# Two tensors that TensorE reads, begun 64 bytes further on in a float32 kernel of eight layers

## The reference, cut to what matters

```python
y = x32 * lax.rsqrt(jnp.mean(x32 * x32, axis=-1, keepdims=True) + EPS)
...
return (jax.nn.silu(h @ wg) * (h @ wu)) @ wd          # feed-forward, 1024 -> 2816 -> 1024
...
proj = jnp.einsum("bsd,de->bse", h, w_in)             # hybrid layer, 1024 -> 3584
...
return x + jnp.einsum("bse,ed->bsd", y, w_out)
```

## Time and profile before

| | |
|---|---|
| median of 3 runs | 1328.5 us (1327.9 to 1328.56) |
| the profiled execution's own time | 1327.45 us |
| its span, first to last instruction | 1325.7 us |
| granted TensorE clock, mean | 0.994 of full speed (2.4 GHz) |
| TensorE matmul busy | 98% of the span |
| DVE, ACT, POOL busy | 68%, 53%, 12% |

### The profile page before, as it was taken

The page is one execution under the profiler, slowest core; times in us unless marked ns, Lnnn a source line. Parts: engine busy times, 40 slices in busy tenths (PEclk is TensorE's granted clock), DMA queues, the critical chain, the costliest instruction groups (busy, mean ns, idle before and its releaser), DMA issues.

```text
span 1325.7 us, 23603 instructions
## 1 busy us (share of the span) xinstructions
PE 1297.9 (98%) x9662; PEld 1219.8 (92%) x9662; DVE 901.2 (68%) x1588; ACT 709.0 (53%) x1149; POOL 153.5 (12%) x207
## 2 busy tenths in 40 slices
PE   9999899999999999999999999999999999999997
PEld 7788678999999988899999999999998889999997
DVE  6986698777665567867666566666547776766652
ACT  7663656564445476466444444454458545554441
POOL 3106510250000210003000011000110001200000
PEclk9999899999999999999999999999999999999999
DMA  8535443555555543245555655555655234555560
GB/s 320 192 106 170 158 168 114 186 175 180 189 190 177 191 146 125 90 132 194 182 179 180 203 180 191 186 179 177 203 164 175 65 128 128 193 177 188 182 198 35
DMA packets 61499, 221.77 MB, mean 167 GB/s; under 512 B 7120, under 2 KB 7376, under 8 KB 61136
## 3 DMA queue, kind: packets, MB, share of 16 engines
q1 hardware_dynamic: 60768, 219.00, 49.8%
q0 software_dynamic: 336, 1.11, 0.3%
q10 hardware_dynamic: 288, 0.16, 0.1%
HBM read 219.20 MB, written 1.05 MB: 166 GB/s over the span
## 4 chain that ended last, share of the span: by engine, by line
PE 80%; DVE 10%; POOL 4%; issue 3%; ACT 1%; DMA 1%; SPq 0%; DVEq 0%; ACTq 0%; POOLq 0%
PE pb L473 13%; PE pb L474 12%; PE pb L475 12%; PE pb L488 7%; PE pb L489 7%; PE pb L490 7%; PE pb L457 5%; PE pb L458 5%; PE pb L459 5%; DVE s_wl L1263 3%; DVE s_acc L1396 2%; PE pb L581 2%; PE pb L531 2%; PE pb L704 1%; PE pb L560 1%
## 5 line engine op out<-in xcount | busy, mean ns | idle before, releaser
L1263 DVE TENSOR_TENSOR s_wl<-s_wraw,s_wh 128x1024 fp32r<-128x1024 f32 (+1 forms) x411 | 505.6, 1251 | 114.4 <-ACT s_wh L882 114.3
L882 ACT ACTIVATE s_wh<-s_wraw 128x1024 fp32r<-128x1024 f32 (+1 forms) x411 | 420.5, 1047 | 199.3 <-PE pb L475 112.6
L473 PE MATMUL pb<-s_xh,s_wh 128*128 128x256 f32 x1408 | 399.5, 284 | 0.0
L475 PE MATMUL pb<-s_xh,s_wl 128*128 128x256 f32 x1408 | 398.8, 283 | 0.0
L474 PE MATMUL pb<-s_xl,s_wh 128*128 128x256 f32 x1408 | 398.8, 283 | 0.0
L474 PEld LDWEIGHTS pb<-s_xl,s_wh 128*128 128x128 f32 x1408 | 270.6, 192 | 0.0
L473 PEld LDWEIGHTS pb<-s_xh,s_wh 128*128 128x128 f32 x1408 | 270.5, 192 | 0.0
L475 PEld LDWEIGHTS pb<-s_xh,s_wl 128*128 128x128 f32 x1408 | 270.5, 192 | 0.0
L488 PE MATMUL pb<-s_hh,s_wh 128*128 128x256 f32 x704 | 194.8, 277 | 0.0
L490 PE MATMUL pb<-s_hh,s_wl 128*128 128x256 f32 x704 | 194.7, 277 | 0.0
L489 PE MATMUL pb<-s_hl,s_wh 128*128 128x256 f32 x704 | 194.7, 277 | 0.0
(11 more groups left out here) (302 smaller groups left out, 1516.2 us busy)
## 6 DMA issues: line engine op xcount, KB each, us to landing
s_wraw<-in_w SPq DMA_DIRECT2D x407, 512.0 KB, 4.1
s_nab<-in_rpb SPq DMA_DIRECT2D x2, 1024.0 KB, 9.4
s_x<-in_x SPq DMA_DIRECT2D x4, 256.0 KB, 5.9
out_dram<-s_at_s SPq DMA_DIRECT2D x4, 256.0 KB, 2.3
s_cst<-in_cst SPq DMA_DIRECT2D x1, 684.0 KB, 9.7
s_mlev<-in_lev POOLq DMA_DIRECT2D x1, 576.0 KB, 5.5
s_wraw<-in_w SPq DMA_DIRECT2D x2, 256.0 KB, 4.4
s_ln<-in_lng POOLq DMA_DIRECT2D x2, 128.0 KB, 7.0
```

The lines of the kernel that those rows point to most:

```text
L473: pe.matmul(o, wh[:, s, w], xh[:, k, :], start=k == v == 0, stop=False, skip_group_check=True)
L475: r = pe.matmul(o, wl[:, s, w], xh[:, k, :], start=False, stop=k == 7, skip_group_check=True)
L882: return act.activation(o, src, ACT.Copy, scale=scale)
L1263: dve.tensor_tensor(wl[:, s, part], wraw[:, r, part], wh[:, s, part].bitcast(F32), ALU.subtract).then_inc(low_done, 1)
```

## The change

Two unused tensors of 16 float32 are taken in the same memory, one ahead of `xh` and one behind `xl`:

```diff
     x = sb("x", [P, 8, TOKENS])
+    sb("gap0", [P, 16])
     xh = sb("xh", [P, 8, TOKENS], F32R)
     xl = sb("xl", [P, 8, TOKENS], F32R)
+    sb("gap1", [P, 16])
     cst = sb("cst", [P, NCST])
```

## The result

| | before | changed |
|---|---|---|
| median us | 1328.2 (4 runs, 1327.69 to 1328.56) | 1319.2 (4 runs, 1317.65 to 1320.94) |
| ratio | 1 | 0.9933, 95% interval 0.9916 to 0.995 |
| profiled execution: span | 1325.7 | 1319.1 |

What follows compares the result with a forecast made beforehand. TensorE's matmul-to-matmul distance was taken to bound the kernel. From 1327.45 us, 26.7 off for project_features after give-backs and 2.7 off for project_tokens gave 1298.0 us, 1299 at the median; range 1292 to 1321.

Steps and rivals of the forecast that it cites:

- The reading of the address: TensorE matmuls: held and moved operand reads collide when both start in the same half of 128 bytes, costing 6.7 ns each.
- The period of 128 bytes: Operand start addresses: only the remainder by 128 bytes counts, so shifting a tensor by 128 bytes costs nothing.
- Step 1: project_features: 4,224 matmuls go from 120.0 to 113.3 ns apart, saving 28.3 us.
- The second state: project_out sometimes ran near 118 ns instead of 113 after an interruption; 113 was expected behind spread's transposes in project_features.
- step 3: Between norm_sums and spread in the feed-forward layers: 120 matmuls run at 118 ns, 0.5 us less gain.
- The 118 state: Rival, chance 0.12: after norm_sums all of project_features runs at 118 ns, saving 8.3 us, giving 1320 us.
- Step 2: Start of feed-forward layers: norm_sums waits for POOL's sum, which gets no faster; together 1.1 us of gain given back.
- Step 4: project_tokens in b1 and mix: 6.7 ns less per matmul, mostly covered by other waits, 2.7 us gained.
- the other bound: project_tokens: 6.7 ns more for each of 1,344 matmuls, 9.0 us worse.
- Step 5: Everything from cst on moves by 128 bytes, and ACT's and DVE's writes of xh and xl change: no cost.
- The slower rival: Chance 0.08: pattern repeats after 256 bytes, project_out falls to 120 ns, 19.3 us lost, project_features gains nothing; 1348 us.
- Step 6: Weight supply and DVE in project_features keep up at the new pace, 2.72 us per weight unit; no new wait.

Runs made afterwards that it cites:

- x at 192: Against the kernel before, xh and xl start 192 bytes further on and everything behind xl 256 bytes further on; 1315.91 us, ratio 0.9908.
- its split: Against the kernel before, parts of xh and xl moved 192 bytes in the feed-forward layers alone, everything behind by 512; 1308.83 us, ratio 0.9864.
- wiping: Parts of xh and xl moved 192 bytes in feed-forward layers alone, but block 7 of 8 kept at distance 0 from wh and wl; 1306.96 us, ratio 0.9837.
- 32 bytes: Against the kernel before, xh and xl start 32 bytes further on and everything behind xl 256 bytes further on; 1322.4 us, ratio 0.9957.
- wiping with distance 64: As wiping, but blocks 0 to 6 of xh and xl at distance 64 from wh and wl in place of 192; 1320.29 us, ratio 0.9944.
- the kernel without the stop: As wiping, with norm_sums after 9 tiles in place of 7 and the spreads after 14 in place of 11, first feed-forward layer; 1301.93 us, ratio 0.9799.
- the first split: Parts of xh and xl at remainder 64 in feed-forward layers alone, 0 in b1 and mix; xl landed 128 bytes off xh by 256; 1322.11 us, ratio 0.9959.
- both wiping kernels: The two kernels wiping and the kernel without the stop, both with block 7 at distance 0; 1306.96 us and 1301.93 us.

## Why the prediction was right or wrong

In the profiled execution the forecast, 1298.0 us, was missed by 22.9 us. By the tables, 11.4 of them are in project_features (26.7 forecast behind steps 1 to 3, 15.3 measured), 7.1 in the stages of b1 and mix (2.7 gained by forecast, 4.4 lost), 4.0 in project_out of the feed-forward layers, which was to stay as it was.

**The reading of the address** was right in kind: equal remainders cost 120 ns, others less, shown from both sides, by x (moved away from 0) and by hh (moved to 0, 119.9 ns). That the relation of the two starts counts, and not the moved one alone, was right as well (the weights moved). The period of 128 bytes was wrong: distance 128 gives 118.6 ns, not the 120 of distance 0. With hh moved by 256 bytes, project_out behind distance 128 stayed at 113.3. A collision of two reads as the reason is argued, not shown: no run looks inside.

The Trainium skill, TensorE: Matmul & The Clock Gate, Step-by-step: what each phase is for, says that the weight load takes no read bandwidth from the running matmul. The prediction drew from it that no start address could matter, and that does not hold here: the same code with hh and y moved by 64 bytes took 17 us more. Whether the sentence itself fails, or something beside bandwidth makes the address count, no run shows.

**Step 1**, 28.3 us for project_features, was sized as if 113.3 ns belonged to the address. It belongs to the address and to a state. Two of four layers had it; the stage gave 15.3 us in the profiled execution. The two layers at 118 cost some 2 x 1,056 x 4.5 ns = 9.5 us, the fall of the clock 2.7.

**The second state** is where the forecast broke, in the sentence on which step 1 rests and by which step 3 limits the 118 ns to 120 matmuls: "In project_features the transposes of `spread` come last, so I expect 113 behind them." That rule was drawn from a handful of stretches of project_out. The runs showed 118 ns behind `spread` in two of four layers, and in the second profile of the same program in two of four again, but not the same two. The program does not fix the choice, it goes as if by chance, and the layer keeps it. The 118 state was seen, priced at 8.3 us and given 0.12, as a case in which all layers have it. Its 1320 is near the 1319.2 measured by luck: it holds one gain of 8.3 us, where the profile has 15.3 in project_features and 8.4 lost elsewhere.

**Step 2**, what is given back at norm_sums, did not count the clock. The wait for POOL in the first feed-forward layer, forecast at 2.2 to 2.3 us, was 1.56 in the changed kernel, whose first layer was at 118; it was 2.2 in the three kernels with that layer's first tiles at 113 (x at 192, its split, and wiping). But behind it the clock fell in the changed kernel's profiled execution: 2.7 us, where 0.56 were allowed for. It fell again in the changed kernel's second profile, and in 7 of the 10 other kernels that had the stop. In the three others (the weights moved, 32 bytes, and wiping with distance 64) TensorE stood still for 1.4 to 1.9 us without a fall. In the kernel without the stop it did not fall.

**Step 4** had its sign wrong. I took the gain of 6.7 ns; the price is 233.2 - 227 = 6.2 ns, near the other bound. Cost on the path: 3.6 us of 1,344 x 6.2 = 8.3, where the 402 matmuls that the step counts as uncovered would give 2.5: cover was judged somewhat too high. The reason given ("the excess there equals that of project_features") did not hold: with 512 columns the distance 192, good for 256 columns, is the bad one.

**Step 5**, everything behind xl, was costed at nothing "as the remainder by 128 stays". Alone it costs 10 us. The slower rival was built on just this, a period of 256, and had half of it right: hh did leave 113, for 118 and not for 120, and only because it came behind x at distance 0. In the changed kernel it inherits x's state, so a loss showed in two layers of four: the 4.0 us of the table. Whether the 128 bytes caused these 4.0 is open. With x and hh both at 192 project_out inherited 118 in the same way; behind an x at 64 and xl at 192 (the first split) it was at 113 in all four layers. No run has all of xh and xl at 64 and hh at its old 192.

**Step 6**, cover at the new pace, was right: weights, DVE and ACT kept up at 113.3 ns.

The range held the median, and partly by luck: its upper end of 1321 was set by another account of the time, and single runs of the changed kernel went up to 1325.53. The direction was right, the size was three times too large.

What stays open: what the two states are inside TensorE, what picks one, why distance 0 has only one, and why 512 columns order the distances differently: project_tokens also holds x and moves the weights, and no run tells the two apart. The clock's fall also has no rule from these runs: the kernel before stood still for 1.7 us without it, and with hh and y at 0 it fell behind 1.17 us.

## What to carry to other kernels

Where TensorE is the bound and every matmul loads new weights, as here, the start addresses of the held and the moved operand can be a parameter of the kernel: count matmuls in a long stretch for each stage and compare stages of one shape. A tensor taken or left out anywhere ahead shifts all that lie behind it, so compare two versions only with their addresses in hand. A result that spreads wider than before is a hint to look for states in the trace, layer by layer, ahead of any mean.

## What the runs showed of the hardware that I had not expected

- At distances 64 and 192 the time from start to start of the same matmul has two stable levels, 113.3 and 117.8 ns, at the same addresses and clock. In these profiles it stays at one of them for 1,500 matmuls and changes only at an interruption or at a change of addresses.
- The order matters: behind 12 matmuls at distance 0 the next 84 were in the 113 state at 192 (both wiping kernels, all layers), and in the 118 state at 64 (one kernel, all layers). Behind 512-column matmuls at distance 0 the state at 192 was the other one.
- A stop of 1.2 to 2.2 us was often, not always, followed by 15 to 31 matmuls at 1.2 GHz, small ones counted; giving TensorE work in its place was worth 5.0 us by the medians and 3.7 in the profiled executions.
